# Two-column bank clears, norm sums without dummies ahead, a signal per output, split LRU output pieces, and final products in pairs

## The chip, the cores and the metric

The kernel runs on one core of one Trainium2 chip. The metric is the device time of one execution in microseconds (us). The profile is of one such execution, taken by the hardware profiler, and its times count from the start of its span.

## What is computed

Two blocks are applied one after the other to a sequence of 256 tokens of width 1024, in float32. The first is a conformer convolution and a state-space branch with gates, then a gated FFN. The second is the one that most of the change touches. Cut to what matters:

```python
h = rms_norm_2(x, norm1_g)
z = h @ w_in                       # lru_x, lru_gate, sc_b, sc_c, sc_x
y_lru = rg_lru(causal_dwconv(lru_x, lru_conv_w) + lru_conv_b, ...) * gelu(lru_gate)   # 1024 wide
y_sc = sc_b * causal_dwconv(sc_c * sc_x, sc_conv_w)                                   # 512 wide
x = x + concatenate([y_lru, y_sc]) @ w_out
h = rms_norm_2(x, norm2_g)
u = causal_dwconv(h @ w_up, ffn_conv_w)
x = x + (gelu(u[:, :3072]) * u[:, 3072:]) @ w_down
return rms_norm_2(x, final_g)
```

`rms_norm_2` divides a token by the root of the mean of its squares, so it needs a sum over all 1024 channels of the finished `x`. The first block ends its mixer and its FFN in the same way, with a norm of the branch's output before it is added to `x`.

## The kernel before, in words

Channels lie on the 128 partitions and tokens on the free axis, so `x` is eight chunks of 128x256. The weights are a stream of 290 **pieces** of 128x1024 (512 KB, eight 128x128 tiles each). SyncE loads them in a fixed order into a ring of eight slots `raw`. A piece is used in one of two ways.

* A **split** piece: ScalarE copies it to `w_hi` (L804, a rounded copy in `float32r`), VectorE subtracts to `w_lo` (L1191), and TensorE multiplies each tile three times (L393 to L395, `h_lo*w_hi`, `h_hi*w_hi`, `h_hi*w_lo`), where the operand is split in the same manner into `h_hi` and `h_lo`. Six pieces are split ahead of the one in use (`LEAD`).
* A **native** piece: TensorE multiplies the tile of `raw` as float32 (L743, L755). The profile shows two records for each such matmul. The set `NATIVE` says which pieces these are. SyncE may load over a split piece's slot when its `w_lo` is made, and over a native one's only when TensorE has finished it.

All orders are written out by hand: each engine has its own program, and semaphores tie them. `pieces_done` counts pieces that TensorE has finished, `lo_ready` the split ones that VectorE has made.

**Output projections** sum into the four PSUM banks of `B`, two outputs of 256 columns in each (`acc_out(m)`). `clear_accumulators` (L421) opens the banks with four zero matmuls of 512 columns and `start=True`; all that follow have `start=False`. It is called four times: in the state-space stage, before the first FFN's down projection, before the output projection of the second block, and before its down projection.

**The output projection of the second block** is pieces `OUT2` = 206 to 217: four for the 512 channels of `sc` (L743), then eight for the 1024 channels of `lru` (L755), one for each output chunk m. All twelve are native. When output m is finished, VectorE adds it to `x` (L1787) and ScalarE squares it (L1035). Between two of these adds both engines split a piece of the FFN that follows, whose pieces begin at `UP2` = 218.

**The first FFN's down projection** ends with six pieces that hold six tiles for each of the eight outputs, so that most outputs end inside a piece. ScalarE copies and squares an output (L1022, L1023) when the piece in which it ends is finished.

**The norm of a token** goes through `spread_residual`. VectorE has added the squares of chunks 0 to 5 into `sq_sum`. TensorE clears two columns (L437), sums `sq_sum` over the partitions (L440), runs `ahead` dummy matmuls of zeros (L488), waits for the squares of chunks 6 and 7 and adds them (L446), runs four dummies, and after VectorE's mean (L1201) and GpSimd's power of -1/2 (L376) spreads the factor over the partitions (L480), with `after` more dummies behind it. It is called four times: behind the mixer of the first block, behind its FFN, behind the output projection of the second block, and at the end.

**The end**: VectorE makes output chunks 0 to 4 from `x`, the gain and the factor in PSUM (L1859), each stored by SyncE (L362). ScalarE weights chunks 5 to 7 (L1169), GpSimd multiplies them by the factor (L383), and ScalarE stores them (L1174).

Of the kernel before, what the change touches and what calls it, by code (L numbers as in the profile page):

```python
# [78 lines left out]
NATIVE = frozenset(GLU_NATIVE) | frozenset([LOOP0 + 8 * i + n for i in range(GROUPS - 1) for n in OUT_AT]) | frozenset(range(TAIL0, PW0)) | frozenset(range(OUT2, UP2))  # L79
# [79 lines left out]
def hybrid_kernel(nc, x_in, weights, params_in, w_dt, lru_w, consts, out):  # L159
    cs_dram = nc.dram_tensor("cs_dram", [HEADS + HPG, T], F32).ap()  # L160
    stack = ExitStack()
    with stack:
# [99 lines left out]

        def out2_done(m):

            return OUT2 + KSC + m + 1
# [14 lines left out]
        DVE_OUT = 5  # L280
        out_weighted = stage[:, 0, :], stage[:, 1, :], stage2[:, 0, :]
# [46 lines left out]
        out_ready, stored = sem("out_ready"), sem("stored")  # L328
        weighted, pool_out = sem("weighted"), sem("pool_out")
# [13 lines left out]
        def _(sp_):  # L343
# [15 lines left out]

            for c in range(DVE_OUT):  # L360
                sp_.wait_ge(out_ready, c + 1)
                sp_.dma_start(out[:, c, :], m_wide[:, c, :]).then_inc(stored, 16)  # L362
            sp_.wait_ge(stored, 16 * KD)
# [3 lines left out]
        def _(pool):  # L367
# [13 lines left out]
            for c in range(DVE_OUT, KD):  # L381
                pool.wait_ge(weighted, c - DVE_OUT + 1)
                nc.gpsimd.tensor_tensor(m_wide[:, c, :], out_weighted[c - DVE_OUT], rs, ALU.mult).then_inc(pool_out, 1)  # L383


        @block.tensor
        def _(pe):
# [30 lines left out]
            def clear_accumulators():  # L418

                for b in range(4):  # L420
                    mm(B[:, b, :], zero[:, :], zero[:, :].unsqueeze(1).to_broadcast([P, 4, P]), start=True,  # L421
                       stop=False, skip_group_check=True)
# [11 lines left out]
            def spread_residual(summed_n, norm_n, squares_n, bank, ahead, after=8, norm_bank=A[3]):  # L434
# [7 lines left out]
                stay_clocked(bank, ahead)  # L442
# [202 lines left out]
            spread_residual(3, 11, 2 * KD, B[:, 0, :], 2, norm_bank=B[:, 3, :])  # L645
# [48 lines left out]
            spread_residual(5, 13, 4 * KD, A[2][:, :], 2)  # L694
# [52 lines left out]
            for m in range(KD):  # L747
                p = OUT2 + KSC + m
                native_loaded(p)
                if m >= 4:  # L750
                    pe.wait_ge(x_new, 2 * KD + m - 3)
                for k in range(KD):
                    if m == 0:
                        pe.wait_ge(lru_ready, k + 1)
                    ins = mm(acc_out(m), raw[:, p % RING, k * P:(k + 1) * P], lru[:, k, :], start=False, stop=False,  # L755
                             skip_group_check=True)
                ins.then_inc(pieces_done, 1)
            spread_residual(7, 15, 6 * KD, A[2][:, :], 4, 5)
# [26 lines left out]
            spread_residual(8, 16, 7 * KD, A[2][:, :], 4, 0)  # L785
# [1200 lines left out]
```

## Time and profile before

| | |
|---|---|
| median of 3 runs | 949.2 us (949.17 to 949.22) |
| time of the profiled execution | 949.5 us |
| its span | 947.7 us |
| TensorE matmul, busy | 935.1 us (99%) |
| VectorE, busy | 720.0 us (76%) |
| ScalarE, busy | 523.2 us (55%) |
| GpSimd, busy | 17.1 us (2%) |
| mean granted TensorE clock | 0.999 |

The span is from the first to the last instruction; the profiled execution's own time is 1.8 us more. A matmul row has a start and a modelled length, and rows overlap, since matmuls are pipelined: what one costs in a row of them is the distance from its start to the next one's start.

### The profile page before, as it was taken

The page shows a single profiled execution, that of the slowest core. Times are in us where ns is not written, and L with a number is a line of the kernel's source. Part 1 is how long each engine was busy: PE and PEld are TensorE (multiplying, and loading weights), DVE is VectorE, ACT ScalarE, POOL GpSimd, SP SyncE. Part 2 cuts the span into 40 slices and gives each one's busy share as a digit, 9 for nine tenths or more (in the row PEclk, how much of TensorE's full clock was granted, in tenths as well). Part 3 has the DMA queues.
Part 4 walks back from the last instruction along what each step waited for, and adds up shares of the span by engine and source line. Part 5 has one row for each costly group of instructions (what it writes and reads, how often), then busy time and mean ns, then how long its engine had stood idle before and what let it go on. Part 6 is the DMA issues. An engine that isn't in the chain of part 4 may idle for free.

```text
span 947.7 us, 19332 instructions
## 1 busy us (share of the span) xinstructions
PE 935.1 (99%) x7228; PEld 905.7 (96%) x7228; DVE 720.0 (76%) x1297; ACT 523.2 (55%) x871; POOL 17.1 (2%) x27
## 2 busy tenths in 40 slices
PE   9999999999999999999999999999999999999997
PEld 7999999999999999999999999999988999999997
DVE  5999999999999888677767445898615888888432
ACT  5547666777667475555554434577213656656331
POOL 0000000000000000000000000000000000000001
PEclk9999999999999999999999999999999999999999
DMA  7576334544544557256555555346046555555601
GB/s 303 181 247 204 127 120 170 199 154 157 193 130 165 201 197 239 98 189 234 179 186 186 174 184 178 112 158 198 25 154 221 192 185 179 181 187 182 204 0 45
DMA packets 45324, 161.54 MB, mean 170 GB/s; under 512 B 5172, under 2 KB 6360, under 8 KB 45144
## 3 DMA queue, kind: packets, MB, share of 16 engines
q1 hardware_dynamic: 43200, 154.61, 48.5%
q10 hardware_dynamic: 2072, 6.21, 1.9%
q8 instruction: 35, 0.57, 0.2%
q14 instruction: 17, 0.14, 0.0%
HBM read 159.72 MB, written 1.09 MB: 170 GB/s over the span
## 4 chain that ended last, share of the span: by engine, by line
PE 63%; issue 24%; DVE 9%; ACT 2%; DMA 1%; POOL 0%; DVEq 0%; ACTq 0%; SPq 0%; POOLq 0%
PE A L393 11%; PE A L394 10%; PE A L395 10%; PE B L393 5%; PE B L395 5%; PE B L394 5%; PE B L588 5%; PE B L755 3%; DVE w_lo L1191 2%; DVE part L1227 2%; PE B L743 1%; DVE acc L1430 1%; ACT dec L906 1%; PE A L569 1%; DMA raw<-in_weights_dram 1%
## 5 line engine op out<-in xcount | busy, mean ns | idle before, releaser
L1191 DVE TENSOR_TENSOR w_lo<-raw,w_hi 128x1024 fp32r<-128x1024 f32 x257 | 312.8, 1222 | 98.2 <-ACT w_hi L804 95.9
L804 ACT ACTIVATE w_hi<-raw 128x1024 fp32r<-128x1024 f32 x257 | 268.8, 1054 | 134.6 <-PE B L395 75.1
L393 PE MATMUL A<-h_lo,w_hi 128*128 128x256 f32 x1176 | 338.0, 287 | 3.2 <-DVE h_lo L1586 1.6
L394 PE MATMUL A<-h_hi,w_hi 128*128 128x256 f32 x1176 | 332.8, 283 | 0.0
L395 PE MATMUL A<-h_hi,w_lo 128*128 128x256 f32 x1176 | 332.8, 283 | 0.0
L393 PEld LDWEIGHTS A<-h_lo,w_hi 128*128 128x128 f32 x1176 | 225.3, 192 | 6.0 <-issue 3.8
L394 PEld LDWEIGHTS A<-h_hi,w_hi 128*128 128x128 f32 x1176 | 225.5, 192 | 0.2
L395 PEld LDWEIGHTS A<-h_hi,w_lo 128*128 128x128 f32 x1176 | 225.3, 192 | 0.0
L393 PE MATMUL B<-h_lo,w_hi 128*128 128x256 f32 x448 | 128.0, 286 | 0.4 <-DVE h_lo L1196 0.4
L394 PE MATMUL B<-h_hi,w_hi 128*128 128x256 f32 x448 | 126.8, 283 | 0.0
L395 PE MATMUL B<-h_hi,w_lo 128*128 128x256 f32 x448 | 126.8, 283 | 0.0
L395 PE MATMUL B<-hid_hi,w_lo 128*128 (+1 forms) x368 | 104.2, 283 | 0.0
L393 PE MATMUL B<-hid_lo,w_hi 128*128 (+1 forms) x368 | 104.0, 283 | 0.0
L394 PE MATMUL B<-hid_hi,w_hi 128*128 (+1 forms) x368 | 103.2, 280 | 0.0
L393 PEld LDWEIGHTS B<-h_lo,w_hi 128*128 128x128 f32 x448 | 86.0, 192 | 0.9 <-issue 0.8
L394 PEld LDWEIGHTS B<-h_hi,w_hi 128*128 128x128 f32 x448 | 86.0, 192 | 0.1
L395 PEld LDWEIGHTS B<-h_hi,w_lo 128*128 128x128 f32 x448 | 86.0, 192 | 0.0
L1227 DVE SCALAR_TENSOR_TENSOR part<-v,par,part 128x256 f32<-128x256 f32 x184 | 76.0, 479 | 0.0
L394 PEld LDWEIGHTS B<-hid_hi,w_hi 128*128 128x128 f32 x368 | 70.0, 190 | 0.1
L393 PEld LDWEIGHTS B<-hid_lo,w_hi 128*128 128x128 f32 x368 | 69.1, 188 | 0.1
L395 PEld LDWEIGHTS B<-hid_hi,w_lo 128*128 128x128 f32 x368 | 68.8, 187 | 0.0
L588 PE MATMUL B<-yn,raw 128*128 128x256 f32 x256 | 58.0, 379 | 0.0
(243 smaller groups left out, 1093.8 us busy)
## 6 DMA issues: line engine op xcount, KB each, us to landing
raw<-in_weights_dram SPq DMA_DIRECT2D x290, 512.0 KB, 4.0
csrow<-cs_dram ACTq DMA_DIRECT2D x9, 512.0 KB, 4.2
x<-in_x_dram SPq DMA_DIRECT2D x2, 512.0 KB, 5.1
bd<-in_lru_w_dram ACTq DMA_DIRECT2D x1, 1024.0 KB, 4.8
out_dram<-m_wide SPq DMA_DIRECT2D x5, 128.0 KB, 2.2
out_dram<-m_wide ACTq DMA_DIRECT2D x3, 128.0 KB, 2.3
par<-in_params_dram SPq DMA_DIRECT2D x1, 379.0 KB, 7.3
cst<-in_consts_dram SPq DMA_DIRECT2D x1, 320.0 KB, 7.5
```

Of the source, the lines that this page charges most:

```text
L393: mm(dst, wh, lo, start=first, stop=False, skip_group_check=free)
L394: mm(dst, wh, hi, start=False, stop=False, skip_group_check=free)
L395: return mm(dst, wl, hi, start=False, stop=last, skip_group_check=free)
L569: mm(A[3][rows, at:at + T], xdt[:, 0, r, :], dec[:, r, 0:T], start=True, stop=False)
L588: ins = mm(acc_out(m), raw[:, p % RING, m * P:(m + 1) * P], yn[:, c, :], start=False, stop=False, skip_group_check=True)
L743: ins = mm(acc_out(m), raw[:, p % RING, n % 8 * P:(n % 8 + 1) * P], sc[:, k, :], start=False, stop=False, skip_group_check=True)
L755: ins = mm(acc_out(m), raw[:, p % RING, k * P:(k + 1) * P], lru[:, k, :], start=False, stop=False, skip_group_check=True)
L804: F(w_hi[:, s, :], raw[:, s, :], ACT.Copy).then_inc(hi_ready, 1)
L906: n = own.up(F(dec[:, r_, b * P:(b + 1) * P], csrow[:, r_, cols], ACT.Relu, bias=cs, scale=-1.0))
L1191: V.tensor_tensor(w_lo[:, s, :], raw[:, s, :], w_hi[:, s, :].bitcast(F32), ALU.subtract).then_inc(lo_ready, 1)
L1227: ins = V.scalar_tensor_tensor(dst, vs(k), w(k), dst, ALU.mult, ALU.add)
L1430: last[c] = own.up(V.scalar_tensor_tensor(acc[:, c, :], v[:, c, k:k + T], col("conv_dw_w", c * CONV_K + k), acc[:, c, :], ALU.mult, ALU.add))
```

## The change

It has five parts.

1. `clear_accumulators` opens each bank with a float32 matmul of two columns in place of one of 512 columns.
2. `spread_residual` loses the dummies `ahead` of the sums of chunks 6 and 7 (2, 2, 4 and 4 of them at the four calls).
3. In the first FFN's down projection the outputs that end inside a piece get a signal of their own, `output_done`, for which ScalarE waits.
4. The eight `lru` pieces of the output projection are split in place of native. ScalarE and VectorE split pieces 210 to 217 and the operand `lru` (into `h_hi` and `h_lo`), and TensorE runs three matmuls for a tile.
5. At the end ScalarE weights all eight chunks behind their squares, VectorE multiplies six of them by the factor in pairs of 512 columns, GpSimd two, and SyncE stores 256 KB at a time.

```diff
-NATIVE = frozenset(GLU_NATIVE) | ... | frozenset(range(TAIL0, PW0)) | frozenset(range(OUT2, UP2))
+NATIVE = frozenset(GLU_NATIVE) | ... | frozenset(range(TAIL0, PW0)) | frozenset(range(OUT2, OUT2 + KSC))
...
+        def ends_piece(m):
+            return (DOWN1_REST * m + DOWN1_REST) % 8 == 0
+        def outputs_ended(m):
+            return sum(not ends_piece(q) for q in range(m + 1))
...
-        DVE_OUT = 5
-        out_weighted = stage[:, 0, :], stage[:, 1, :], stage2[:, 0, :]
+        DVE_OUT = 6
...
-            for c in range(DVE_OUT):
-                sp_.wait_ge(out_ready, c + 1)
-                sp_.dma_start(out[:, c, :], m_wide[:, c, :]).then_inc(stored, 16)
-            sp_.wait_ge(stored, 16 * KD)
+            for c in range(0, DVE_OUT, 2):
+                sp_.wait_ge(out_ready, c // 2 + 1)
+                sp_.dma_start(out[:, c:c + 2, :], m_wide[:, c:c + 2, :]).then_inc(stored, 16)
+            sp_.wait_ge(stored, 16 * (DVE_OUT // 2 + KD - DVE_OUT))
...
-                pool.wait_ge(weighted, c - DVE_OUT + 1)
-                nc.gpsimd.tensor_tensor(m_wide[:, c, :], out_weighted[c - DVE_OUT], rs, ALU.mult).then_inc(pool_out, 1)
+                pool.wait_ge(weighted, c + 1)
+                nc.gpsimd.tensor_tensor(m_wide[:, c, :], m_wide[:, c, :], rs, ALU.mult).then_inc(pool_out, 1)
...
-                    mm(B[:, b, :], zero[:, :], zero[:, :].unsqueeze(1).to_broadcast([P, 4, P]), start=True,
-                       stop=False, skip_group_check=True)
+                    mm(B[:, b, 0:TT], zero[:, :].bitcast(F32), zero[:, 0:TT].bitcast(F32), start=True, stop=False,
+                       skip_group_check=True)
...
-            def spread_residual(summed_n, norm_n, squares_n, bank, ahead, after=8, norm_bank=A[3]):
+            def spread_residual(summed_n, norm_n, squares_n, bank, after=8, norm_bank=A[3]):
...
-                stay_clocked(bank, ahead)
                 for c in (KD - 2, KD - 1):
...
                 if n % 8 == 7:
                     ins.then_inc(pieces_done, 1)
-            spread_residual(5, 13, 4 * KD, A[2][:, :], 2)
+                elif k == DOWN1_REST - 1:
+                    ins.then_inc(output_done, 1)
+            spread_residual(5, 13, 4 * KD, A[2][:, :])
...
-                native_loaded(p)
+                pe.wait_ge(lo_ready, split_order(p))
...
-                        pe.wait_ge(lru_ready, k + 1)
-                    ins = mm(acc_out(m), raw[:, p % RING, k * P:(k + 1) * P], lru[:, k, :], start=False, stop=False,
-                             skip_group_check=True)
+                        pe.wait_ge(operand_ready, ops + k + 1)
+                    ins = tile(p % RING, k, h_hi[:, k, :], h_lo[:, k, :], acc_out(m), False, False, True)
                 ins.then_inc(pieces_done, 1)
-            spread_residual(7, 15, 6 * KD, A[2][:, :], 4, 5)
+            ops += KD
+            spread_residual(7, 15, 6 * KD, A[2][:, :], 5)
...
-                act.wait_ge(pieces_done, down1_done(m))
+                if ends_piece(m):
+                    act.wait_ge(pieces_done, down1_done(m))
+                else:
+                    act.wait_ge(output_done, outputs_ended(m))
...
+            for p in range(OUT2 + KSC, OUT2 + LEAD):
+                split_hi(p)
+            act.wait_ge(pieces_done, OUT2)
+            for c in range(KD):
+                act.wait_ge(lru_ready, c + 1)
+                F(h_hi[:, c, :], lru[:, c, :], ACT.Copy).then_inc(stage_hi, 1)
             residual_squares(2 * KD, OUT2, UP2)
...
-            residual_squares(3 * KD)
-            for c in range(DVE_OUT, KD):
-                F(out_weighted[c - DVE_OUT], x[:, c, :], ACT.Identity, scale=col("final_g_2", c)).then_inc(weighted, 1)
+            for c in range(KD):
+                act.wait_ge(x_new, 3 * KD + c + 1)
+                F(sq_wide[:, c, 0:T], x[:, c, :], ACT.Square).then_inc(squares_ready, 1)
+                F(m_wide[:, c, :], x[:, c, :], ACT.Identity, scale=col("final_g_2", c)).then_inc(weighted, 1)
...
+            dve.wait_ge(lru_ready, KD)
+            for p in range(OUT2 + KSC, OUT2 + LEAD):
+                split_lo(p)
+            for c in range(KD):
+                operand_low(hi_n + c, lru[:, c, :], h_hi[:, c, :], h_lo[:, c, :])
+            hi_n += KD
...
-            dve.wait_ge(x_new, 4 * KD)
-            for c in range(DVE_OUT):
-                V.scalar_tensor_tensor(m_wide[:, c, :], x[:, c, :], col("final_g_2", c), rstd, ALU.mult,
-                                       ALU.mult).then_inc(out_ready, 1)
+            for c in range(0, DVE_OUT, 2):
+                dve.wait_ge(weighted, c + 2)
+                V.tensor_tensor(m_wide[:, c:c + 2, :], m_wide[:, c:c + 2, :], rstd.unsqueeze(1).to_broadcast([P, 2, T]),
+                                ALU.mult).then_inc(out_ready, 1)
```

The order of instructions moves at three places. The first is VectorE at the output projection of the second block. Before, the last products of the LRU branch are followed at once by the add of output 0:

```order
L1761 TENSOR_TENSOR lru<-sq_wide,stage 128x256 [waits gelu_ready,dve_steps] x2
L1787 TENSOR_TENSOR x<-x,B 128x256 [waits pieces_done]
L1191 TENSOR_TENSOR w_lo<-raw,w_hi 128x1024 [waits hi_ready]
L1787 TENSOR_TENSOR x<-x,B 128x256 [waits pieces_done]
L1191 TENSOR_TENSOR w_lo<-raw,w_hi 128x1024 [waits hi_ready]
```

And now (L1210 is the weight split, L1215 the operand's low part, L1812 the add to `x`):

```order
L1780 TENSOR_TENSOR lru<-sq_wide,stage 128x256 [waits gelu_ready,dve_steps] x2
L1210 TENSOR_TENSOR w_lo<-raw,w_hi 128x1024 [waits hi_ready,lru_ready]
L1210 TENSOR_TENSOR w_lo<-raw,w_hi 128x1024 [waits hi_ready]
L1215 TENSOR_TENSOR h_lo<-lru,h_hi 128x256 [waits stage_hi] x8
L1210 TENSOR_TENSOR w_lo<-raw,w_hi 128x1024 [waits hi_ready] x6
L1812 TENSOR_TENSOR x<-x,B 128x256 [waits pieces_done]
L1210 TENSOR_TENSOR w_lo<-raw,w_hi 128x1024 [waits hi_ready]
```

Eight weight splits and eight operand parts stand ahead of the first add now, and six of the splits stand between the operand and that add.

The second place is ScalarE at the same point. Before, the eight gelus of the gate are followed by the square of output 0:

```order
L1121 ACTIVATE stage<-stage 128x256 [waits scaled] x8
L1035 ACTIVATE sq_wide<-x 128x256 [waits x_new]
L804 ACTIVATE w_hi<-raw 128x1024 [waits pieces_done,loaded2]
L1035 ACTIVATE sq_wide<-x 128x256 [waits x_new]
L804 ACTIVATE w_hi<-raw 128x1024 [waits pieces_done,loaded3]
```

And now (L813 is the weight copy, L1139 the operand's high part, L1044 the square):

```order
L1133 ACTIVATE stage<-stage 128x256 [waits scaled] x8
L813 ACTIVATE w_hi<-raw 128x1024 [waits pieces_done,loaded2]
L813 ACTIVATE w_hi<-raw 128x1024 [waits pieces_done,loaded3]
L1139 ACTIVATE h_hi<-lru 128x256 [waits lru_ready,pieces_done]
L1139 ACTIVATE h_hi<-lru 128x256 [waits lru_ready] x7
L813 ACTIVATE w_hi<-raw 128x1024 [waits pieces_done,loaded4]
L813 ACTIVATE w_hi<-raw 128x1024 [waits pieces_done,loaded5]
L813 ACTIVATE w_hi<-raw 128x1024 [waits pieces_done,loaded6]
L813 ACTIVATE w_hi<-raw 128x1024 [waits pieces_done,loaded7]
L813 ACTIVATE w_hi<-raw 128x1024 [waits pieces_done,loaded0]
L813 ACTIVATE w_hi<-raw 128x1024 [waits pieces_done,loaded1]
L1044 ACTIVATE sq_wide<-x 128x256 [waits x_new]
```

The last of these copies is of piece 217, in slot 1 of the ring, and it waits for the load of that piece.

The third place is TensorE at the norm behind this projection. Before:

```order
L437 MATMUL A<-zero 128x2 [waits squares_summed]
L440 MATMUL A<-cst,sq_sum 128x1 x2
L488 MATMUL A<-zero 128x512 x4
L446 MATMUL A<-cst,sq_wide 128x1 [waits squares_ready]
L446 MATMUL A<-cst,sq_wide 128x1
```

And now:

```order
L445 MATMUL A<-zero 128x2 [waits squares_summed]
L448 MATMUL A<-cst,sq_sum 128x1 x2
L453 MATMUL A<-cst,sq_wide 128x1 [waits squares_ready]
L453 MATMUL A<-cst,sq_wide 128x1
L453 MATMUL A<-cst,sq_wide 128x1 [waits squares_ready]
```

The four dummies between the sum of chunks 0 to 5 and that of chunk 6 are gone; the waits are the same.

## Rows read from the trace of the kernel before

**Rows 1.** The page's engine totals: busy time, share, instructions.

```profile
PE 935.1 (99%) x7228; PEld 905.7 (96%) x7228; DVE 720.0 (76%) x1297; ACT 523.2 (55%) x871; POOL 17.1 (2%) x27
```

**Rows 2.** TensorE's waits: us in total, times, longest; its largest.

```profile
PE A L393 <- DVE h_lo L1586: 1.6, 2, 0.8
```

**Rows 3.** Timeline, TensorE, a clear: start us, us, engine line operation, count.

```profile
521.84 0.28 PE L395 MATMUL A<-h_hi,w_lo 128*128 128x256 f32 x1
521.96 1.09 PE L421 MATMUL B<-zero 128*128 128x512 f32 x4
522.89 0.28 PE L393 MATMUL B<-hid_lo,w_hi 128*128 x1
```

**Rows 4.** Timeline, TensorE, the norm behind the first FFN.

```profile
586.25 0.28 PE L437 MATMUL A<-zero 128*128 128x2 f32 x2
586.38 0.58 PE L440 MATMUL A<-cst,sq_sum 128*128 128x1 f32 x4
586.83 0.71 PE L488 MATMUL A<-zero 128*128 128x512 f32 x2
587.38 0.28 PE L446 MATMUL A<-cst,sq_wide 128*128 128x1 f32 x2
```

**Rows 5.** Timeline, TensorE, from a native matmul to split ones.

```profile
618.21 0.47 PE L393 MATMUL A<-h_lo,w_hi 128*128 128x256 f32 x1
618.52 0.28 PE L394 MATMUL A<-h_hi,w_hi 128*128 128x256 f32 x1
```

**Rows 6.** Timeline, ScalarE, squares of chunks 6 and 7, first FFN.

```profile
586.44 0.38 ACT L1022 ACTIVATE sq_wide<-B 128x256 f32<-128x256 f32 x1 [2.21 <-PE B L395]
...
586.99 0.39 ACT L1022 ACTIVATE sq_wide<-B 128x256 f32<-128x256 f32 x1
```

**Rows 7.** Timeline, TensorE, output projection of the second block and its norm.

```profile
681.12 1.09 PE L421 MATMUL B<-zero 128*128 128x512 f32 x4
682.06 13.98 PE L743 MATMUL B<-sc,raw 128*128 128x256 f32 x64
695.87 27.79 PE L755 MATMUL B<-lru,raw 128*128 128x256 f32 x128
723.50 0.28 PE L437 MATMUL A<-zero 128*128 128x2 f32 x2
...
724.08 1.17 PE L488 MATMUL A<-zero 128*128 128x512 f32 x4
725.09 0.95 PE L446 MATMUL A<-cst,sq_wide 128*128 128x1 f32 x8
```

**Rows 8.** Timeline, VectorE, adds and weight splits; idle before in brackets.

```profile
699.52 0.42 DVE L1787 TENSOR_TENSOR x<-x,B 128x256 f32<-128x256 f32 x1 [16.53 <-PE B L755]
...
708.90 0.42 DVE L1787 TENSOR_TENSOR x<-x,B 128x256 f32<-128x256 f32 x1
710.79 1.23 DVE L1191 TENSOR_TENSOR w_lo<-raw,w_hi 128x1024 fp32r<-128x1024 f32 x1 [1.48 <-ACT w_hi L804]
711.93 0.41 DVE L1787 TENSOR_TENSOR x<-x,B 128x256 f32<-128x256 f32 x1
```

**Rows 9.** Timeline, ScalarE, the same place.

```profile
703.18 1.06 ACT L804 ACTIVATE w_hi<-raw 128x1024 fp32r<-128x1024 f32 x1 [2.78 <-DMA raw<-in_weights_dram]
...
724.15 0.42 ACT L1035 ACTIVATE sq_wide<-x 128x256 f32<-128x256 f32 x1 [3.04 <-DVE x L1787]
```

**Rows 10.** Timeline, TensorE, the dummies ahead at the last norm.

```profile
938.26 1.17 PE L488 MATMUL A<-zero 128*128 128x512 f32 x4
```

**Rows 11.** Single lines: duration of one in ns, min/median/max.

```profile
L1406 DVE TENSOR_TENSOR y<-y,zs x8: 691/692/694, 105.9 to 305.6; 128x512 f32<-128x512 f32 x8
```

**Rows 12.** Timeline, the end: VectorE's and GpSimd's products.

```profile
941.99 2.05 DVE L1859 SCALAR_TENSOR_TENSOR m_wide<-x,par,A 128x256 f32<-128x256 f32 x5 [1.57 <-PE A L480]
942.89 2.10 POOL L383 TENSOR_TENSOR m_wide<-stage,mean 128x256 f32<-128x256 f32 x3 [1.71 <-ACT mean L1171]
```

**Rows 13.** Windows of the end; last three columns: PEclk, DMA share, GB/s.

```profile
945.80:946.20 0.40, 0.00 (x0) 0.00 (x0) 0.00 (x0) 0.00 (x0) 0.00 (x0) 0.77 1.04 348
```

More of the change, by code:

```diff
@@ L78 @@
 GLU_NATIVE = (0, 1, 2, 5, 9)
-NATIVE = frozenset(GLU_NATIVE) | frozenset([LOOP0 + 8 * i + n for i in range(GROUPS - 1) for n in OUT_AT]) | frozenset(range(TAIL0, PW0)) | frozenset(range(OUT2, UP2))
+NATIVE = frozenset(GLU_NATIVE) | frozenset([LOOP0 + 8 * i + n for i in range(GROUPS - 1) for n in OUT_AT]) | frozenset(range(TAIL0, PW0)) | frozenset(range(OUT2, OUT2 + KSC))
 UP1_TURNS = 2 * KF // RING
@@ L328, in hybrid_kernel @@
         out_ready, stored = sem("out_ready"), sem("stored")
+        output_done = sem("output_done")
         weighted, pool_out = sem("weighted"), sem("pool_out")
@@ L644, in _ @@
                 chunk_piece(MIX0 + m, 0, ring_bank(72 + m), h_hi, h_lo)
-            spread_residual(3, 11, 2 * KD, B[:, 0, :], 2, norm_bank=B[:, 3, :])
+            spread_residual(3, 11, 2 * KD, B[:, 0, :], norm_bank=B[:, 3, :])
             scaled_four(UP1, 2 * KD, 4, 12, UP1_BANKS, B[:, 3, :])
@@ L784, in _ @@
                 ins.then_inc(pieces_done, 1)
-            spread_residual(8, 16, 7 * KD, A[2][:, :], 4, 0)
+            spread_residual(8, 16, 7 * KD, A[2][:, :], 0)
             for t in range(TT):
```

## The prediction

> **What bounds the kernel now.** I read the engine totals first: TensorE's matmuls are busy for 935.1 us, 99% of the 947.7 us span, and VectorE for 76% [rows 1]. A busy engine could still be pacing itself on others, so the second view is TensorE's own waits: the largest sum of one kind is 1.6 us, in two waits, among 7228 matmuls [rows 2]. So TensorE is the path nearly throughout, and a microsecond taken from its stream is a microsecond off the end, as long as no other engine then becomes late. The third view is therefore the timeline of TensorE at each edited place, where the distance from start to start is what an instruction costs. The fourth is the timeline of VectorE and ScalarE at the same places, for how much they have in hand. The end is a tail of its own: after the last spread of the factor only products and stores are left [rows 12].
>
> **Part 1, the clears.** Four zero matmuls of 512 columns take 521.96 to 522.89, so 0.93 us [rows 3]; before the second block's projection 681.12 to 682.06, 0.94 [rows 7]. I price the other two calls alike: 3.7 us in all. A float32 matmul of two columns is not free: the clear of two columns and the two sums ahead of the dummies, three such matmuls (the float32 ones have two records each), take 586.25 to 586.83, 0.58 us, or 0.193 each [rows 4]. Four cost 0.77. There is also a price for going from native to split matmuls: 618.21 to 618.52 is 0.31, where a split matmul takes 0.12 (521.84 to 521.96), so 0.19 more [rows 3, 5]. At three of the four places split matmuls follow. The gain of a call is 0.93 − 0.77 = 0.16 without that price, −0.03 with it. If the small ones could be hidden as plain columns they would cost nearly nothing, and the gain of four would be up to 3; against that, these small matmuls already cost 0.193 in a row in this trace. I take 0.2 for all four, bounds −0.2 and 1.3 (a third of the cost hidden).
>
> The Trainium skill ("TensorE: Matmul & The Clock Gate", sections "LDWEIGHTS" and "Weight-path perf modes") has a weight load at P/1.2 ns, 107 ns for 128 columns, and says that the fast load doesn't serve float32. Two passes for each of four such clears would be an estimate of 0.85 us by that page, and part 1 would be worth 0.1 a call or less: it speaks against this part, and the rows agree nearly.
>
> **Parts 2 and 3, the dummies ahead.** Behind the first FFN two of them take 586.83 to 587.38, 0.55 [rows 4]; the call behind the first mixer has two as well, 0.55. The call behind the second projection has four, 724.08 to 725.09, 1.01 [rows 7], and the last one has four too [rows 10]. Removed, they are 3.1 us of TensorE. But the sums behind them wait for squares. At the second projection the square of chunk 7 is from 724.15 to 724.57 [rows 9], while its pair of matmuls would be reached at 724.08 + 0.4 = 724.48: with some 0.08 for the signal it starts at 724.65 instead of 725.09 + 0.4 = 725.49, a gain of 0.84. The last call has the same four and the same order, so again 0.8. Behind the first FFN the square of chunk 7 ends at 587.38 [rows 6]. Sums that start at 586.83 would wait at chunk 7 from 587.22, which leaves 0.38; with signals of their own the outputs before it are fetched as they end, and the 0.55 is whole. Sum 0.55 + 0.55 + 0.8 + 0.8 = 2.7, bounds 1.9 (each call loses 0.2 to a square) and 3.1.
>
> **Part 4, the split pieces.** The 64 native tiles take 695.87 to 723.50, 27.63 us, 0.432 each [rows 7]. A split tile is three matmuls of 0.12, 0.36 [rows 3]. 64 × (0.432 − 0.36) = 4.6 us, less the 0.19 for the step from native to split [rows 5]: 4.4, bounds 4.2 and 4.6. It holds only if weights and operand are there in time. VectorE is idle for 16.53 us before the add at 699.52, that is from 682.99, when the last `lru` is made [rows 8]. From there it has two weight splits at 1.23 and eight operand parts at some 0.4 (the duration of an add of the same shape): ready at 682.99 + 2.5 + 3.2 = 688.6. The first `lru` tile is due at 695.87: 7 us of cover. If that cover were gone, each us would cost a us. ScalarE's part of each is shorter (1.06 and 0.4) and lies ahead of VectorE's.
>
> The load of a piece takes long: output 0 is finished at 699.52, which frees the slot of piece 210 for 218, and ScalarE's copy of 218 waits for that load until 703.18, 3.66 us [rows 8, 9]. Piece 217 goes where the last `sc` piece was, free at 695.87, so it lands at 699.5, its copy ends at 700.6 and its split at 701.9. Since that split stands ahead of the add of output 0 in VectorE's new order, this add comes at 701.9, where before it came at 699.5 and TensorE is then done at 698.9. From there ScalarE and VectorE run in a lap: add, square, copy, split, add. From 708.90 to 711.93 that lap takes 3.03 [rows 8], more than TensorE's 8 × 0.36 = 2.88. Five laps bring output 5 to 717.1 and two last adds without splits, with their sums of squares some 0.9 each, output 7 to some 718.9. TensorE ends output 7 at 695.87 + 0.19 + 64 × 0.36 = 719.1. So by these rows TensorE is still the later, by about 0.2 us: nearly a tie, and the first rival. The weights of the FFN are no new load: its split pieces run at 2.88 a piece before and after.
>
> **Part 5, the tail.** VectorE's five products take 941.99 to 944.04, GpSimd's three 942.89 to 944.99 [rows 12]. After it VectorE has three of 128x512; a product of that shape takes 0.69 [rows 11]: 2.0 in a row, as before, the first one 0.2 later, since it makes two chunks. GpSimd has two in place of three, 0.7 less. But near the end the stores are what counts: from 945.8 to 946.2, the last product long made, the DMA share is 1.04 at 348 GB/s [rows 13]. A megabyte at 348 GB/s is 3.0 us. Larger stores could move at most a little faster, and the last to start is earlier by up to 0.7. I take 0.3, bounds 0 and 0.75.
>
> **Sum.** 0.2 + 2.7 + 4.4 + 0.3 = 7.6 us. Of the profiled execution's 949.5 that leaves 941.9; the median of the runs is 0.3 below it, 949.2, so the forecast is 941.6.
>
> **Rivals.** A, the lap wins at the projection: if the load of 217 is later than 3.66 us (seven loads are queued behind it at once now, since split pieces free their slots early), or the lap is longer than 3.03, output 7 is added late and the norm with it. Its price is the delay less the 0.2: 1.5 us of delay gives 942.9, 2.8 gives 944.2. For it: the tie above, and a wait on a load in the rows; against it: queued loads follow 217 and don't go ahead of it. A delay that eats all of part 4 would need 4.6 us, 946.0.
>
> B, slower than before: the clock. The dummies may be what holds TensorE's clock through the four norms. The granted clock is near 1.00 throughout and falls to the lower level (1.2 GHz) only at the end, 0.77 on average from 945.8 to 946.2 with the products begun at 941.99 [rows 13, 12], so some 4 us after the last matmuls. At the lower level every us of work costs a second one. A norm without the dummies ahead has still nearly no idle time, 0.2 us where a square is late, against the 4 that the row shows; I see no gap that would do it. It decides once 7.6 us are lost, that is 15.2 us of time at half clock over the four calls; 20 us at it would give 951.6. The Trainium skill ("TensorE: Matmul & The Clock Gate", section "HAM oscillation — how this bites in real kernels") tells of kernels that fall to the low clock again and again for waits between short bursts; by it any fall would show as a granted clock of 0.5 behind a norm.
>
> C, more: small clears partly hidden and the tail at its best bound, 0.8 + 0.4 more, 940.4 or less.
>
> D, the change doesn't do what it says: the dummies were covering a wait on squares that stays, and the clears cost what they did; 4.4 + 1 is left, 944.
>
> **How the numbers follow.** The forecast's case (940.6 to 942.6) 0.68; A up to 944.2 0.12; A worse or D, 944 to 948, 0.07; C 0.08; B 0.05. The range takes in the forecast, A and most of C: 940.0 to 944.2. A difference under 0.2%, 1.9 us, I call no change: faster is under 947.3. Faster 0.68 + 0.12 + 0.08 + most of the 0.07 = 0.94; the same 0.03 (a part of A and of B); slower 0.03.
>
> **What would show it.** In the changed kernel's trace: `lru`'s 64 tiles in 23.0 to 23.3 us instead of 27.63; two operand and weight waits on TensorE at nearly nothing before the first of them; the add of output 0 at about 701.5, adds then 3.0 apart, and no idle on TensorE over 0.2 us between output 7's end and chunk 7's sum; a clear of 0.7 to 0.9; the start of the last sums 0.8 nearer to the last product; stores that end 4.5 us or so behind the first output product. Wrong it would be if a clear cost under 0.4 (then 2 us more come), if the adds of the projection are late (A), if the granted clock falls behind a norm (B), or if the stores' end hangs on something other than their rate.

## The result, and the profile after

The changed kernel takes 941.87 us (median of 4 runs, 941.68 to 941.99) against 949.21 before: 7.3 us less, ratio 0.9921 (95% interval 0.991 to 0.9933). The profiled execution took 941.99 us, its span is 940.2, 7.5 less than the span before.

The page's engine totals of the changed kernel. TensorE is still busy for 99% of the span, VectorE and ScalarE carry 12 us more each.

```profile
PE 928.0 (99%) x7296; PEld 902.9 (96%) x7296; DVE 731.8 (78%) x1311; ACT 535.6 (57%) x892; POOL 16.4 (2%) x26
```

TensorE's waits (us in total, times, longest). The largest is the one of before [rows 2]. L1215 makes every operand's low part, the new one of `lru` too, but its row is no new wait: it is TensorE's at the first tile behind the third norm (722.87), and the kernel before has the same wait there, of 0.4:

```profile
PE A L401 <- DVE h_lo L1605: 1.6, 2, 0.8
PE B L401 <- DVE h_lo L1215: 0.4, 1, 0.4
```

The row of the kernel before:

```profile
PE B L393 <- DVE h_lo L1196: 0.4, 1, 0.4
```

The new operand is in time. VectorE makes its eight low parts until 687.26, and TensorE's first `lru` tile starts at 694.61:

```profile
684.49 2.77 DVE L1215 TENSOR_TENSOR h_lo<-lru,h_hi 128x256 fp32r<-128x256 f32 x8
```

The timeline of TensorE, a clear (L429), to be held against [rows 3]. Two-column float32 clears show eight records, two for each matmul.

```profile
521.41 0.95 PE L429 MATMUL B<-zero 128*128 128x2 f32 x8
522.22 0.37 PE L401 MATMUL B<-hid_lo,w_hi 128*128 x1
522.43 0.28 PE L402 MATMUL B<-hid_hi,w_hi 128*128 x1
```

From start to start it is 0.81, in place of 0.93, but the first matmul behind it takes 0.21 where it took 0.12 behind the wide clear, so that 0.03 is gained. The timeline of TensorE at the norm behind the first FFN, against [rows 4]:

```profile
585.66 0.28 PE L445 MATMUL A<-zero 128*128 128x2 f32 x2
585.80 0.58 PE L448 MATMUL A<-cst,sq_sum 128*128 128x1 f32 x4
586.25 1.03 PE L453 MATMUL A<-cst,sq_wide 128*128 128x1 f32 x8
587.14 1.16 PE L495 MATMUL A<-zero 128*128 128x512 f32 x4
```

The sums of chunks 6 and 7 follow at once on those of `sq_sum`. They take 0.89 where they took 0.80 behind the dummies (587.38 to 588.18), so that about 0.45 of the dummies' 0.55 is gained. The same timeline at the second block's output projection and its norm, against [rows 7]:

```profile
680.09 0.95 PE L429 MATMUL B<-zero 128*128 128x2 f32 x8
680.89 14.06 PE L752 MATMUL B<-sc,raw 128*128 128x256 f32 x64
...
694.61 0.47 PE L401 MATMUL B<-h_lo,w_hi 128*128 128x256 f32 x1
...
717.83 0.28 PE L445 MATMUL A<-zero 128*128 128x2 f32 x2
717.97 0.58 PE L448 MATMUL A<-cst,sq_sum 128*128 128x1 f32 x4
718.41 1.15 PE L453 MATMUL A<-cst,sq_wide 128*128 128x1 f32 x8
719.42 1.18 PE L495 MATMUL A<-zero 128*128 128x512 f32 x4
```

The 64 `lru` tiles take 23.22 us in place of 27.63. The adds of that projection on VectorE (L1812; the first, then the last ones) and the last step of the sum of squares (L1272), against [rows 8]:

```profile
700.23 0.41 DVE L1812 TENSOR_TENSOR x<-x,B 128x256 f32<-128x256 f32 x1
...
715.23 0.41 DVE L1812 TENSOR_TENSOR x<-x,B 128x256 f32<-128x256 f32 x1
...
716.68 0.42 DVE L1272 TENSOR_TENSOR sq_sum<-sq_sum 128x256 f32<-128x256 f32 x1
718.03 0.42 DVE L1812 TENSOR_TENSOR x<-x,B 128x256 f32<-128x256 f32 x1 [0.92 <-PE B L403]
```

The adds of outputs 0 to 5 are 3.0 apart (five laps from 700.23 to 715.23): the lap of ScalarE and VectorE sets their pace. But before the add of output 7 VectorE stands idle for 0.92 us and waits for TensorE: the lap is in time, with 0.92 us in hand. ScalarE at the same place, the copy of piece 217 and the square of chunk 7:

```profile
698.00 1.06 ACT L813 ACTIVATE w_hi<-raw 128x1024 fp32r<-128x1024 f32 x1 [2.38 <-DMA raw<-in_weights_dram]
...
718.48 0.42 ACT L1044 ACTIVATE sq_wide<-x 128x256 f32<-128x256 f32 x1 [1.72 <-DVE x L1812]
```

Last the end: the products of VectorE and GpSimd, and a window (the last three columns are the granted clock, DMA share and GB/s), against [rows 12, 13].

```profile
934.68 1.88 DVE L1884 TENSOR_TENSOR m_wide<-m_wide,A 128x512 f32<-128x512 f32 x3 [1.57 <-PE A L487]
935.59 1.41 POOL L391 TENSOR_TENSOR m_wide<-m_wide,mean 128x256 f32<-128x256 f32 x2 [1.71 <-ACT mean L1190]
```

```profile
938.00:939.00 1.00, 0.00 (x0) 0.00 (x0) 0.00 (x0) 0.00 (x0) 0.00 (x0) 1.00 1.04 370
```

**Where the 7.5 us came from**, by the distances between the same marks in the two traces: the four norms up to their next dummies 0.47, 0.45, 0.81 and 0.81; from the third clear to the end of the `lru` tiles 4.64; the other three clears with all that follows them 0.01, 0.04 and 0.04; the end, from the dummies behind the last sums, 0.19; and 0.07 from the first weights, which landed earlier. Between these places the two kernels run alike to 0.02.

### The profile page after: what moved, and what is told of

It reads as the page before. It is cut to its first block, busy times and chain, and to the rows that moved or that the text cites. A ratio compares the mean times of both kernels' runs of the same rounds, so it can differ in the third digit from the quotient of the medians.

```text
span 940.2 us, 19509 instructions
## 1 busy us (share of the span) xinstructions
PE 928.0 (99%) x7296; PEld 902.9 (96%) x7296; DVE 731.8 (78%) x1311; ACT 535.6 (57%) x892; POOL 16.4 (2%) x26
## 4 chain that ended last, share of the span: by engine, by line
PE 63%; issue 24%; DVE 9%; ACT 2%; DMA 1%; POOL 0%; DVEq 0%; ACTq 0%; SPq 0%; POOLq 0%
PE A L401 11%; PE A L402 10%; PE A L403 10%; PE B L403 6%; PE B L401 6%; PE B L402 6%; PE B L595 5%; DVE w_lo L1210 2%; DVE part L1246 2%; PE B L752 1%; DVE acc L1449 1%; ACT dec L915 1%; PE A L576 1%; DMA raw<-in_weights_dram 1%; DVE dec L1412 1%
## 5 line engine op out<-in xcount | busy, mean ns | idle before, releaser
L1210 DVE TENSOR_TENSOR w_lo<-raw,w_hi 128x1024 fp32r<-128x1024 f32 x265 | 322.4, 1222 | 99.1 <-ACT w_hi L813 96.8
L813 ACT ACTIVATE w_hi<-raw 128x1024 fp32r<-128x1024 f32 x265 | 277.1, 1053 | 140.6 <-PE B L403 75.9
L401 PE MATMUL B<-h_lo,w_hi 128*128 128x256 f32 x512 | 146.2, 286 | 0.4 <-DVE h_lo L1215 0.4
L402 PE MATMUL B<-h_hi,w_hi 128*128 128x256 f32 x512 | 144.9, 283 | 0.0
L403 PE MATMUL B<-h_hi,w_lo 128*128 128x256 f32 x512 | 144.9, 283 | 0.0
L401 PEld LDWEIGHTS B<-h_lo,w_hi 128*128 128x128 f32 x512 | 98.2, 192 | 1.0 <-issue 0.8
L402 PEld LDWEIGHTS B<-h_hi,w_hi 128*128 128x128 f32 x512 | 98.3, 192 | 0.1
L403 PEld LDWEIGHTS B<-h_hi,w_lo 128*128 128x128 f32 x512 | 98.2, 192 | 0.0
```

The lines of the kernel that those rows point to most:

```text
L401: mm(dst, wh, lo, start=first, stop=False, skip_group_check=free)
L402: mm(dst, wh, hi, start=False, stop=False, skip_group_check=free)
L403: return mm(dst, wl, hi, start=False, stop=last, skip_group_check=free)
L813: F(w_hi[:, s, :], raw[:, s, :], ACT.Copy).then_inc(hi_ready, 1)
L1210: V.tensor_tensor(w_lo[:, s, :], raw[:, s, :], w_hi[:, s, :].bitcast(F32), ALU.subtract).then_inc(lo_ready, 1)
```

## The experiments

All are edits of the changed kernel, and their medians are to be read against its 941.87. The ratio behind each is to the kernel before, in runs on the same chip. On the three chips of the experiments the kernel before took 949.30, 949.35 and 949.21 us, so a difference of 0.1 us between two medians says nothing by itself. An instruction's line can be a few off that of the changed kernel where an edit moved it.

**Part 4 undone.** The set of native pieces reaches to `UP2` again, the loop of the eight pieces is the old one, and the splits of 210 to 217 and of the operand are gone.

```diff
-frozenset(range(OUT2, OUT2 + KSC))
+frozenset(range(OUT2, UP2))
...
-                    ins = tile(p % RING, k, h_hi[:, k, :], h_lo[:, k, :], acc_out(m), False, False, True)
+                    ins = mm(acc_out(m), raw[:, p % RING, k * P:(k + 1) * P], lru[:, k, :], start=False, stop=False,
+                             skip_group_check=True)
```

> The changed kernel with part 4 undone (the eight lru pieces native again, no weight splits and operand parts for them). Theory (every part is worth what it takes from TensorE's stream): 4.4 us longer than the changed kernel's 941.9, so 946.3, the 64 tiles in 27.6 us in place of 23.2. Rival (the lap of ScalarE and VectorE eats a part, the gain came from elsewhere): less than 3 us longer, under 944.9.

Measured: 946.29 us (946.24 to 946.53), 4.4 longer; ratio 0.9968 (0.9956 to 0.998). Its timeline of TensorE, the first `sc` tile, the `lru` tiles and what follows:

```profile
680.84 3.48 PE L752 MATMUL B<-sc,raw 128*128 128x256 f32 x15
...
694.73 27.79 PE L764 MATMUL B<-lru,raw 128*128 128x256 f32 x128
722.36 0.28 PE L445 MATMUL A<-zero 128*128 128x2 f32 x2
```

The tiles take 27.63 again. Part 4 is worth what it takes from TensorE, and the rival falls. From the clear's start (680.02 here) to the norm it is 42.34 against 37.74, so part 4 alone is 4.60.

**Part 2 undone.**

```diff
+                stay_clocked(bank, ahead)
                 for c in (KD - 2, KD - 1):
```

> The changed kernel with the 2, 2, 4 and 4 dummies ahead put back. Theory: 0.47 + 0.45 + 0.8 + 0.8 = 2.5 us longer, 944.4. Rival (the dummies held the clock and so paid for a part of their own time): less than 1.5 us longer, or a granted clock that differs behind a norm.

Measured: 944.42 us (944.33 to 944.52), 2.55 longer; ratio 0.9948 (0.9935 to 0.9962). At the third norm, timeline of TensorE:

```profile
718.72 0.58 PE L448 MATMUL A<-cst,sq_sum 128*128 128x1 f32 x4
719.17 1.19 PE L496 MATMUL A<-zero 128*128 128x512 f32 x4
720.19 0.95 PE L454 MATMUL A<-cst,sq_wide 128*128 128x1 f32 x8
721.00 1.16 PE L496 MATMUL A<-zero 128*128 128x512 f32 x4
```

From L448 to the next dummies 2.28, in the changed kernel 717.97 to 719.42, 1.45. That is 0.83, less than the 1.01 of the dummies (719.17 to 720.19). About half of the rest is the 0.09 that narrow sums cost more directly behind others; for the other half, in the changed kernel the square of chunk 7 ends at 718.90, while its pair of matmuls would be reached at some 718.8 and waits a little for it.

**Part 1 undone** (the four clears 512 columns wide again).

```diff
-                    mm(B[:, b, 0:TT], zero[:, :].bitcast(F32), zero[:, 0:TT].bitcast(F32), start=True, stop=False,
-                       skip_group_check=True)
+                    mm(B[:, b, :], zero[:, :], zero[:, :].unsqueeze(1).to_broadcast([P, 4, P]), start=True,
+                       stop=False, skip_group_check=True)
```

> The changed kernel with the clears of 512 columns put back. Theory (a two-column float32 matmul costs 0.2 us here, nearly what the wide one costs): 0.2 to 0.3 us longer, 942.1. Rival (the small ones hide behind the matmuls that follow): 1 us or more longer, 943 or above.

Measured: 941.81 us (941.81 to 941.90); ratio 0.9921 (0.9907 to 0.9934). No difference to the changed kernel's 941.87, and the rival falls. By the distances between the same marks in the two traces the wide clears cost 0.03, 0.04, 0.03 and 0.04 more, 0.14 in all. Its first weights land 0.28 earlier (TensorE's first matmul on weights at 7.69, in the changed kernel at 7.97), and a start of that kind, which varies from one execution to the next, is more than what is sought. Part 1 as it stands is worth about 0.1 us.

**Part 5 undone** (five products, three on GpSimd, eight stores of 128 KB).

```diff
-        DVE_OUT = 6
+        DVE_OUT = 5
...
-            for c in range(0, DVE_OUT, 2):
-                sp_.wait_ge(out_ready, c // 2 + 1)
-                sp_.dma_start(out[:, c:c + 2, :], m_wide[:, c:c + 2, :]).then_inc(stored, 16)
+            for c in range(DVE_OUT):
+                sp_.wait_ge(out_ready, c + 1)
+                sp_.dma_start(out[:, c, :], m_wide[:, c, :]).then_inc(stored, 16)
```

> The changed kernel with the old end (five products of one chunk on VectorE, three on GpSimd, stores of 128 KB). Theory (the end is bound by the rate of the stores, which is 365 GB/s with 2 KB rows and 340 with 1 KB rows): 0.2 us longer, 942.1, the store rate in the full windows near 340 again. Rival (GpSimd's third product sets the end): 0.7 us longer, 942.6.

Measured: 942.00 us (941.86 to 942.24), 0.13 longer; ratio 0.9922 (0.9909 to 0.9936). Two windows of its end:

```profile
937.00:938.00 1.00, 0.00 (x0) 0.00 (x0) 0.00 (x0) 0.00 (x0) 0.68 (x1) 1.00 1.00 327
938.00:939.00 1.00, 0.00 (x0) 0.00 (x0) 0.00 (x0) 0.00 (x0) 0.00 (x0) 1.00 1.05 343
```

From 938 to 939 the DMA share is 1.05 here and 1.04 in the changed kernel, and it moves 343 GB/s here and 370 with the wider rows. GpSimd's third product ends at 937.7, 0.7 later than its second in the changed kernel, while the span is 0.2 longer: this fits the theory that the store rate sets the end, and not the rival's 0.7. The edit undoes the rows and the third product together, and the difference is small, so it is not shown beyond that.

**Part 3 undone.**

```diff
-                if ends_piece(m):
-                    act.wait_ge(pieces_done, down1_done(m))
-                else:
-                    act.wait_ge(output_done, outputs_ended(m))
+                act.wait_ge(pieces_done, down1_done(m))
```

> The changed kernel with part 3 undone (ScalarE waits for whole pieces again in the first down projection). Theory: chunk 7's square ends some 0.2 us after TensorE would reach its sum, 0.1 to 0.2 us longer, 942.0. Rival (the signals do nothing): no difference, and the sums behind the first FFN start and end as in the changed kernel.

Measured: 942.07 us (941.81 to 942.13), 0.2 longer, which the ranges don't tell from nothing; ratio 0.9924 (0.991 to 0.9937). The trace tells. TensorE behind the first FFN:

```profile
586.28 1.16 PE L453 MATMUL A<-cst,sq_wide 128*128 128x1 f32 x8
587.30 0.93 PE L495 MATMUL A<-zero 128*128 128x512 f32 x3
```

The next dummies stand at 587.30 with the clear of two columns (L445) before them at 585.65, in the changed kernel at 587.14 and 585.66: 0.17 later.

**The lap made longer**, to see how much cover part 4 has.

```diff
+                    if end and c < 6:
+                        for e in range(2):
+                            F(sq_wide[:, c, 0:T], x[:, c, :], ACT.Square).then_inc(twice, 1)
+                            act.wait_ge(twice, 2 * c + e + 1)
                     F(sq_wide[:, c, 0:T], x[:, c, :], ACT.Square).then_inc(squares_ready, 1)
```

> The changed kernel with the squares of outputs 0 to 5 of the second block's projection made three times, each after the last one has ended, which lengthens the lap of ScalarE and VectorE by 0.9 to 1.0 us a time. Theory (the lap has 0.92 us in hand at output 7): five laps make 4.7 us, less 0.9, 3.5 to 4.2 us longer, 945.4 to 946.1. Rival (the lap has more cover than that, or none of it matters): under 2 us longer.

Measured: 949.79 us (949.03 to 949.97), 7.9 longer; ratio 1.0003 (0.9994 to 1.0012). Twice what I expected. Its largest wait of TensorE, and its windows behind the projection (PEclk is the third column from the end):

```profile
PE A L446 <- DVE sq_sum L1277: 4.7, 1, 4.7
```

```profile
720.00:721.00 1.00, 0.00 (x0) 0.00 (x0) 0.78 (x3) 0.82 (x2) 0.00 (x0) 0.92 0.14 49
...
722.00:724.00 2.00, 1.56 (x8) 1.56 (x8) 0.71 (x2) 1.25 (x2) 0.00 (x0) 0.50 0.26 88
...
730.00:731.00 1.00, 1.00 (x6) 0.90 (x5) 1.00 (x4) 0.49 (x2) 0.00 (x0) 0.50 0.07 16
731.00:732.00 1.00, 1.00 (x10) 1.00 (x10) 1.00 (x4) 0.69 (x2) 0.00 (x0) 0.96 0.00 0
```

The lap became 3.9 and the sum of squares was ready at 722.4 in place of 717.1, so TensorE stood idle for 4.7 us. That is the part that the theory had, somewhat undersized: the longer square of output 5 adds to its five laps, since VectorE waits 0.7 us for a square before the last sums. The other 3.2 us is the clock: it fell while TensorE stood idle and stayed at its lower level of 1.2 GHz until 731, for the first 8.6 us after TensorE had begun again. From the norm's clear of two columns to the FFN's first matmul it is 7.8 us there (722.44 to 730.28) and 5.0 in the changed kernel (717.83 to 722.87), and the stretch from there to 731 holds the rest. So a late lap costs its delay and then the clock.

**No dummies in the norms at all.**

```diff
-                stay_clocked(bank, 4)
                 spread_scale(norm_n, norm_bank)
-                stay_clocked(bank, after)
```

> The changed kernel without any dummy in the four norms (neither ahead of the sums, nor before the factor, nor behind it), so that TensorE stands idle for some 1.5 us before the factor and up to 3 us behind it. Theory (these dummies lie in waits and the clock needs longer gaps to fall): within 0.3 us of 941.9, granted clock 1.00 behind each norm. Rival B of the prediction (the dummies hold the clock): the granted clock is 0.5 for a stretch behind a norm and the time is 1 us or more longer for each norm where it falls, 944 to 950.

Measured: 950.09 us (946.64 to 950.50, 11 runs), 8.2 longer; ratio 1.0003 (0.9994 to 1.0012). My theory falls: rival B's mechanism, that dummies hold the clock, is real for these ones. The profile is of the shortest of these runs (946.64), so it shows less of the loss than the median has; its windows behind the first norm:

```profile
391.00:392.00 1.00, 0.00 (x0) 0.00 (x0) 0.97 (x3) 0.20 (x1) 0.00 (x0) 0.73 0.04 16
...
397.00:398.00 1.00, 1.00 (x6) 1.00 (x6) 1.00 (x4) 0.69 (x3) 0.00 (x0) 0.50 0.00 0
```

The clock is at 0.5 from 391.5 to 398.3, and again behind the second and the third norm (593 to 596, 726 to 729). Two gaps stand ahead of it, 1.0 us before the factor and 2.6 behind it. Two more kernels part them.

**Only the four before the factor removed.**

```diff
-                stay_clocked(bank, 4)
                 spread_scale(norm_n, norm_bank)
                 stay_clocked(bank, after)
```

> The changed kernel without the four dummies between the sums and the factor's spread, at all four norms; those behind it stay. TensorE then stands idle for 1.0 us there. If a gap of 1 us does no harm: within 0.2 us of 941.9 and granted clock 1.00 throughout. If the clock falls behind it: 943 or more.

Measured: 943.10 us (942.38 to 943.75), 1.2 longer; ratio 0.9933 (0.9916 to 0.9949). TensorE at the first norm, and the windows there:

```profile
387.57 0.28 PE L445 MATMUL B<-zero 128*128 128x2 f32 x2
387.71 0.58 PE L448 MATMUL B<-cst,sq_sum 128*128 128x1 f32 x4
388.15 1.03 PE L453 MATMUL B<-cst,sq_wide 128*128 128x1 f32 x8
390.20 1.21 PE L486 MATMUL B<-cst,scale 128*128 128x128 f32 x4 [1.02 <-POOL scale L384]
```

```profile
390.00:391.00 1.00, 0.80 (x4) 0.80 (x5) 0.00 (x0) 0.00 (x0) 0.15 (x1) 0.62 0.19 70
391.00:392.00 1.00, 1.00 (x4) 0.87 (x4) 0.52 (x2) 0.00 (x0) 0.00 (x0) 0.50 0.00 0
```

The idle time is 1.0 us, with 1.6 us of matmuls of one or two columns ahead of it, and the clock falls behind it, at all three inner norms, for 3.4 us each. It costs little, since the dummies behind the factor lie in that stretch and have nobody waiting for them.

**Only those behind the factor removed.**

```diff
                 stay_clocked(bank, 4)
                 spread_scale(norm_n, norm_bank)
-                stay_clocked(bank, after)
```

> The changed kernel without the dummies behind the factor's spread (2.6 us idle at the first two norms, 1.6 at the third); those before it stay. If the fall seen without any dummy came from this gap alone: clock 0.5 behind one or more of the norms and 944 to 950. If it took both gaps together: within 0.3 us of 941.9.

Measured: 946.04 us (944.36 to 946.10), 4.2 longer; ratio 0.9961 (0.9947 to 0.9976). The first norm, TensorE's first matmul behind the factor and two windows:

```profile
393.35 0.35 PE L401 MATMUL A<-h_lo,w_hi 128*128 128x256 f32 x1 [2.64 <-DVE h_lo L1604]
```

```profile
394.00:395.00 1.00, 1.00 (x10) 1.00 (x9) 1.00 (x4) 0.79 (x2) 0.00 (x0) 0.92 0.06 16
395.00:396.00 1.00, 1.00 (x7) 1.00 (x6) 1.00 (x4) 0.82 (x2) 0.00 (x0) 0.50 0.00 0
```

The gap of 2.6 alone is enough too, and the fall comes late, 1.5 us after the work has begun again; behind the second norm it comes 0.1 us after, and behind the third, where the gap is only 1.6 us, 0.5 us after. Here it hits work that counts.

How long TensorE stands idle doesn't settle it alone. At the start of the trace of the kernel with part 5 undone, TensorE's first matmul on weights waits longer than the 1.0 and the 1.6 us above:

```profile
7.98 3.72 PE L415 MATMUL A<-v,raw 128*128 128x256 f32 x16 [1.80 <-DMA raw<-in_weights_dram]
```

This gap of 1.8 us stands behind 4.9 us of dummies of 512 columns without a pause, and the granted clock stays at 1.00 in every window from 0 to 16 us. What these runs don't show is how wide, how many and how close the matmuls ahead of a gap must be; narrow sums as a cause of their own were not tested.

**Clears of 128 columns in float32r.**

```diff
-                    mm(B[:, b, 0:TT], zero[:, :].bitcast(F32), zero[:, 0:TT].bitcast(F32), start=True, stop=False,
-                       skip_group_check=True)
+                    mm(B[:, b, 0:P], zero[:, :], zero[:, :], start=True, stop=False, skip_group_check=True)
```

> The changed kernel with each bank opened by one float32r matmul of 128 columns in place of the float32 one of two. Theory (a float32 matmul costs for its two passes and its slow weight load, a float32r one of 128 columns costs 0.06 to 0.12): a call takes 0.25 to 0.5 us in place of 0.8, 1.2 to 2.2 us off four calls, 939.7 to 940.7. Rival (any small matmul costs its 0.2): 941.9.

Measured: 940.28 us (940.08 to 940.51), 1.6 shorter; ratio 0.9906 (0.9891 to 0.9921). The second clear on TensorE:

```profile
520.83 0.56 PE L429 MATMUL B<-zero 128*128 128x128 f32 x4
521.22 0.33 PE L401 MATMUL B<-hid_lo,w_hi 128*128 x1
```

A clear takes 0.39 in place of 0.81. What part 1 was after can be had, but up to 128 columns their number is not what decides: the profile shows eight records for the four float32 matmuls of two columns and four for the float32r ones of 128 columns, and each record costs 0.10 in both.

**No clear at the second block's projection**, the first matmul of outputs 0 to 3 opens its bank.

```diff
-            clear_accumulators()
...
-                ins = mm(acc_out(m), raw[:, p % RING, n % 8 * P:(n % 8 + 1) * P], sc[:, k, :], start=False, stop=False,
+                ins = mm(acc_out(m), raw[:, p % RING, n % 8 * P:(n % 8 + 1) * P], sc[:, k, :], start=m < 4 and k == 0, stop=False,
```

> The changed kernel without the clear ahead of the second block's output projection: the first matmul of outputs 0 to 3 opens its bank. Theory (TensorE is the path, and this clear stands in its stream for 0.80 us): 0.8 us shorter, 941.1. Rival (a small clear overlaps with what follows, so that its removal gives less than its place in the timeline): under 0.4 us, 941.5 or above.

Measured: 940.72 us (940.66 to 940.95), 1.15 shorter; ratio 0.9911 (0.9894 to 0.9927). The profiled executions lie 1.3 apart; of these 0.9 lies between the second and the third norm, and 0.35 is the start again (first matmul on weights at 7.62). The clear is worth at least its 0.80 in the timeline, and the rival falls.

**The three together**, with no clear of two columns ahead of the norms' sums either.

```diff
-                mm(norm_bank[:, 0:TT], zero[:, :].bitcast(F32), zero[:, 0:TT].bitcast(F32), start=True, stop=False,
-                   skip_group_check=True)
                 for t in range(TT):
-                    mm(norm_bank[:, t:t + 1], sq_sum[:, 0, t * P:(t + 1) * P], ones[:, 0:1], start=False, stop=False,
+                    mm(norm_bank[:, t:t + 1], sq_sum[:, 0, t * P:(t + 1) * P], ones[:, 0:1], start=t == 0, stop=False,
```

> Changed kernel with one float32r matmul of 128 columns for a clear (three calls), none ahead of the second block's output projection, and none ahead of the norms' sums (the first sum opens the bank). Theory: the short clears' 1.6 us, 0.4 more at the projection, four times 0.14 to 0.19 at the norms: 939.2 to 939.4. Rival (a wait takes over somewhere): 940 or above.

Measured: 939.31 us (939.15 to 939.58), 2.6 under the changed kernel and 9.9 under the one before; ratio 0.9895 (0.9879 to 0.9912). The theory's 939.2 to 939.4 holds, and no other wait takes over.

## Why the prediction came out

The forecast was 941.6, and 941.87 was measured. The sum had 7.6 us, and the traces show 7.5, so the terms can be held against each other. That the total is so close is in part luck: part 4 came 0.2 above its term, the others together nearly 0.4 below theirs, and 0.07 came from an earlier start that has nothing to do with the change. The mechanism was as described.

* **The bound.** TensorE paces the kernel: each part that was undone alone cost what it takes from TensorE's stream (4.4 for part 4, 2.55 for part 2, 0.2 for part 3, nothing for part 1) or from the end (0.13 for part 5). Part 3's 0.2 may not be added to part 2's 2.55: the signals only let the removed dummies be worth their full 0.45 at that norm. Without it the parts are 7.1 of the 7.3 us measured, and the rest is of the size by which starts and chips differ. That TensorE is the path is shown by parts 4 and 2.
* **Part 4**: predicted 4.4, is 4.60. The step "less the 0.19 for the step from native to split" was wrong in that sum. The longer distance after the first split matmul is there, but that matmul itself starts 0.17 earlier behind the native ones (13.72 from the first `sc` matmul to it, 13.89 with `lru` native): what stands in one distance is missing from the one before. So the step itself costs nothing here.
* **The race in part 4**: I had TensorE as the later one by 0.2 us, "nearly a tie". It was later by 0.7: VectorE was through with the sum of squares at 717.1, and TensorE with output 7 at 717.83, with the signal 0.92 of idle time for VectorE. Two things made the margin larger. The add of output 0 came 5.62 us behind TensorE's first `lru` matmul (694.61 to 700.23) where the prediction had 6.03 (695.87 to 701.9), because load, copy and split of piece 217 took 0.4 less; and the lap was 3.00 and not 3.03, which over five laps is nearly 0.2. The "about 701.5" of the prediction's signs was 1.3 too late: 0.4 for this, and the rest because TensorE's stream stood 1.26 earlier there than before, of which 701.5 had counted 0.4. The mechanism was as described; the chance of rival A was right to be given, and the lengthened lap shows that its price was put too low, since behind the delay comes the clock.
* **Parts 2 and 3**: predicted 2.7, is 2.54, or 2.55 by the runs. The sums of two chunks take 0.89 directly behind the other narrow sums and 0.80 behind wide dummies, and I had taken the full 0.55 where 0.47 and 0.45 came. At the two late squares 0.81 against the 0.84 and 0.8 of the prediction. The signals are worth 0.17, as worked out (the prediction's 0.38 of 0.55 without them).
* **Part 1**: predicted 0.2, is 0.1. The small float32 matmuls cost 0.2 each, nothing of them is hidden, and the bound of 1.3 had no ground. What the matmul behind a clear costs more was put at 0.19 and is 0.09.
* **Part 5**: predicted 0.3, is 0.13 to 0.19. The stores' rate rises from 343 to 370 GB/s, which would be 0.2 us on a megabyte (an estimate from these two rates); what GpSimd ends earlier is not seen at the end, and VectorE's first product comes 0.2 later.
* **Rival B**, the clock: the forecast that the dummies ahead are not what holds it was right, the granted clock stays at 1.00 behind each norm, with them and without. But the ground given, "0.2 us where a square is late, against the 4 that the row shows", was wrong: 1.0 us of idle time behind 1.6 us of narrow sums is enough. Both groups of dummies that stay, before the factor and behind it, are needed for this: without either one the clock falls. So the chance of 0.05 for rival B rested on a margin of 4 us that isn't there; that the change stayed clear of the fall owed something to luck. How near it came, no run shows.

## What to carry to other kernels

Where one engine is busy for 99% of the span, cost every edit by the distance from start to start in its own stream, and check each other engine's lap for who waits at its last turn; errors in the terms of such a sum were here at most 0.2 us. A small matmul is not cheap for having few columns: count its records in the profile, and ask whether the first real matmul can open the bank instead. Here dummies could be taken out where other matmuls follow at once, but beside a wait of 1 us they held the clock; remove them place by place and read the granted clock behind each.

## What the runs showed of the hardware

* The granted clock. At the end of the kernel before it fell at about 946.0, 3.6 us behind the last matmul. Behind a norm it fell after 1.0 us of idle time with matmuls of one and two columns ahead of it, while 1.8 us behind 4.9 us of dummies of 512 columns left it at 1.00. In the kernels with dummies removed it stayed at the lower level for 3.4 us, once for 6.8, and with the lap made longer for 10.2. With the dummies behind the factor removed the fall came 0.1 to 1.5 us after the work had begun again. The Trainium skill ("TensorE: Matmul & The Clock Gate", section "HAM oscillation — how this bites in real kernels") tells of such repeated falls behind waits. The runs without dummies agree with it, with 8.2 us more at the median, but the waits here were shorter (1.0, 1.6 and 2.6 us) than the 3 to 5 us of that page's kernel.
* A float32 matmul of two columns takes 0.20 us in a row of them (clear of the changed kernel), a float32r one of 128 columns 0.10 (short clears), one of 512 columns 0.23 (clear of the kernel before).
* Stores with rows of 2 KB ran at 370 GB/s, with rows of 1 KB at 343, at DMA shares of 1.04 and 1.05.
* The first weights reached TensorE between 7.6 and 8.0 us into the span from one profile to the next, 0.46 us in all, which is more than the worth of each of parts 1, 3 and 5.
